# A mixer block with a product-key expert layer: U and V stages of the experts run as one mixed stage

## Reference

```
q = (h @ peer_wq).reshape(T, 8, 2, 128)
s = einsum('thpd,hpkd->thpk', q, peer_keys)        # 128 scores per head and side
sv, si = top_k(s, 16)
cand = sv[..., 0, :, None] + sv[..., 1, None, :]   # 16 x 16 pairs
top, pos = top_k(cand, 16)                         # 16 experts per head and token
eidx = i * 128 + j of the chosen pair;  g = softmax(top)
a = gelu(einsum('td,thkd->thk', h, peer_u[eidx]))
out = einsum('thkd,thk->td', peer_v[eidx], g * a)
x = x + ga2 * out
```

## Time and profile before

| | |
|---|---|
| median of 3 runs | 1783.68 us (1782.01 to 1784.19) |
| the profiled execution | 1786.27 us |
| its span, first to last instruction | 1784.5 us |
| TensorE busy | 1660.3 us (93%) |
| VectorE busy | 1420.8 us (80%) |
| ScalarE busy | 695.1 us (39%) |
| Pool busy | 607.4 us (34%) |
| moved by DMA | 443.82 MB, mean 249 GB/s |
| TensorE's granted clock, mean | 0.965 |

### The profile page before, as it was taken

The page is one execution under the profiler, slowest core; times in us unless marked ns, Lnnn a source line. Parts: engine busy times, 40 slices in busy tenths (PEclk is TensorE's granted clock), DMA queues, the critical chain, the costliest instruction groups (busy, mean ns, idle before and its releaser), DMA issues.

```text
span 1784.5 us, 29098 instructions
## 1 busy us (share of the span) xinstructions
PE 1660.3 (93%) x9345; PEld 1510.1 (85%) x9345; DVE 1420.8 (80%) x2563; ACT 695.1 (39%) x987; POOL 607.4 (34%) x633
## 2 busy tenths in 40 slices
PE   2899889999899996899898899899999999999998
PEld 1675447887688996798898898899999999999998
DVE  7795646657599999988898898865888888888886
ACT  4331655233434333254454454443333333333331
POOL 2100000101234554555555555541333333333331
PEclk8999789999999998899999999999999999999999
DMA  7521114655322554488898998988999999999996
GB/s 248 175 95 36 60 41 152 222 187 189 118 83 96 178 170 131 153 290 329 320 338 335 336 335 322 357 300 318 341 343 352 349 338 350 354 336 349 354 339 227
DMA packets 182381, 443.82 MB, mean 249 GB/s; under 512 B 13728, under 2 KB 95776, under 8 KB 180656
## 3 DMA queue, kind: packets, MB, share of 16 engines
q1 hardware_dynamic: 118768, 234.91, 38.4%
q0 software_dynamic: 42784, 156.26, 23.6%
q10 hardware_dynamic: 20768, 51.89, 7.8%
HBM read 388.47 MB, written 54.53 MB: 248 GB/s over the span
## 4 chain that ended last, share of the span: by engine, by line
PE 61%; DVE 24%; DMA 7%; issue 4%; ACT 3%; DVEq 0%; POOL 0%; ACTq 0%; POOLq 0%; SPq 0%
PE bank L1528 10%; PE bank L1527 10%; PE bank L1526 10%; PE bank L1278 8%; PE bank L1279 7%; PE bank L1280 7%; DMA sb_x<-u_rows_dram,sb_scr 4%; DVE sb_scr L1081 2%; DVE sb_wide L1184 2%; DVE sb_x L1145 2%; DMA a_scratch<-sb_scr 2%; PE bank L1501 2%; PE bank L1389 1%; DVE sb_scr L829 1%; DVE sb_w_lo L815 1%
## 5 line engine op out<-in xcount | busy, mean ns | idle before, releaser
L1278 PE MATMUL bank<-sb_act_hi,sb_w_hi 128*128 128x384 f32 (+1 forms) x1424 | 511.8, 359 | 14.4 <-POOL sb_w_lo L440 13.6
L1279 PE MATMUL bank<-sb_act_lo,sb_w_hi 128*128 128x384 f32 (+1 forms) x1424 | 503.1, 353 | 0.0
L1280 PE MATMUL bank<-sb_act_hi,sb_w_lo 128*128 128x384 f32 (+1 forms) x1424 | 503.0, 353 | 0.0
L497 ACT ACTIVATE sb_w_hi<-sb_stage 128x1024 fp32r<-128x1024 f32 x324 | 342.3, 1057 | 377.0 <-PE bank L1528 329.4
L815 DVE TENSOR_TENSOR sb_w_lo<-sb_stage,sb_w_hi 128x1024 fp32r<-128x1024 f32 x266 | 324.4, 1220 | 98.8 <-ACT sb_w_hi L497 92.2
L1528 PE MATMUL bank<-sb_mix_hi,sb_w_lo 128*128 128x384 f32 x1024 | 342.0, 334 | 0.0
L1527 PE MATMUL bank<-sb_mix_lo,sb_w_hi 128*128 128x384 f32 x1024 | 342.0, 334 | 0.0
L1526 PE MATMUL bank<-sb_mix_hi,sb_w_hi 128*128 128x384 f32 x1024 | 342.0, 334 | 0.0
L1278 PEld LDWEIGHTS bank<-sb_act_hi,sb_w_hi 128*128 128x128 f32 x1424 | 271.9, 191 | 36.6 <-POOL sb_w_lo L440 15.0
L1279 PEld LDWEIGHTS bank<-sb_act_lo,sb_w_hi 128*128 128x128 f32 x1424 | 271.9, 191 | 15.2 <-issue 0.5
L1280 PEld LDWEIGHTS bank<-sb_act_hi,sb_w_lo 128*128 128x128 f32 x1424 | 270.8, 190 | 15.9
(11 more groups left out here) (192 smaller groups left out, 1767.2 us busy)
## 6 DMA issues: line engine op xcount, KB each, us to landing
sb_stage<-u_dram SPq DMA_DIRECT2D x128, 512.0 KB, 3.9
sb_stage<-v_dram SPq DMA_DIRECT2D x128, 512.0 KB, 6.5
sb_stage<-w_front_dram SPq DMA_DIRECT2D x68, 512.0 KB, 3.3
a_scratch<-sb_scr ACTq DMA_DIRECT2D x128, 192.0 KB, 4.1
g_scratch<-sb_scr ACTq DMA_DIRECT2D x12, 2048.0 KB, 9.6
sb_scr<-g_scratch SPq DMA_DIRECT2D x32, 768.0 KB, 7.9
sb_scr<-a_scratch SPq DMA_DIRECT2D x32, 768.0 KB, 10.6
sb_scr<-w_ada_dram POOLq DMA_DIRECT2D x32, 512.0 KB, 4.4
```

What stands on the lines that cost most here:

```text
L497: nc.scalar.activation(w_hi[:, slot, :], stage[:, slot, :], ACT.Copy).then_inc(w_round, 1)
L1278: nc.tensor.matmul(out, w_hi[:, slot, w], rhs_hi[:, dc, :], start=(i == 0), stop=False)
L1279: nc.tensor.matmul(out, w_hi[:, slot, w], rhs_lo[:, dc, :], start=False, stop=False)
L1280: last = nc.tensor.matmul(out, w_lo[:, slot, w], rhs_hi[:, dc, :], start=False, stop=(i == len(dcs) - 1))
```

## The change

The two expert stages become one mixed stage. The first 64 U slabs (`EARLY`) stay on their own, then one more (`FUSED`); their coefficients still go through `a_scratch`. After that come 64 steps (`STEPS`), each of three units: the V slab of an early U slab, a new U slab (its gelu stays on the core), and the V slab of the new U slab of the step before. Four steps make a lap, for which SP loads G of four old and four new slabs and A of four old ones.

- V slabs are turned round: the coefficients are stationary and 512 weight columns move, 18 matmuls in six banks; the last two banks hold the new U slabs. At the end the three tiles' sums are copied out of PSUM and transposed.
- Pool splits the third unit of each step, VectorE the first two. Before the steps the G turns and the slabs up to `FUSED` + 2 are split by VectorE, as before.
- All gathers but eight move into the steps: four per step (two U rows, two V rows), issued by Pool behind its split, with eight row buffers and the index column read without a copy. Eight early dots are done in slabs 60 to 63. The last four steps have V rows only.
- The top-k is reordered: tiles 0 and 1 first (over all heads), with their lists after slabs 14 and 16, then tiles 2 and 3. The exponential is in slabs 9 and 34, the third list comes after the first G turn.
- G starts after slab 36 and is built in 24 slabs, two batches in each. It is laid out by groups of four slabs, so its store has runs of 512 bytes and its load runs of 6 KB; within a group the four slabs' values of a token lie together.
- `a_scratch` holds 64 slabs, not 128.

The core of the diff:

```diff
+EARLY = 64
+STEPS = SLABS - EARLY
+EXP_SLABS = {9: (0, 1), 34: (2, 3)}
+LIST_SLABS = (14, 16)
+G_FIRST = 36
+G_UNITS = 4
 G_TURNS = ND // (2 * TB)
 G_LAST = G_FIRST + G_TURNS * G_UNITS
 POOL_FIRST, POOL_LAST = WQ0 + 2, FRONT + G_FIRST + 2
-assert LIST_SLABS[-1] + 1 < G_FIRST and G_LAST < SLABS
-
-
-EARLY_SLAB = 28
-G_DOTS = 20
-DOTS_A = G_TURNS * G_DOTS
-LATE_TURNS = (SLABS - 4 - G_LAST) // 4
-LATE_DOTS = PICKS - DOTS_A
+LATE_LIST = DT - 1
+assert G_LAST <= EARLY - 4 and G_FIRST % RING == 0
...
+FUSED = FRONT + EARLY
+STEP0 = FUSED + 1
+LAP = 4
+LAPS = STEPS // LAP
+PICKS_LAP = PICKS // LAPS
+ROWS = 8
+EARLY_DOTS = PICKS_LAP
...
+            def lap_loads(lap, s, first=False, last=False):
+
+                def unit_load(c, src):
+                    slot = (STEP0 + c) % RING
+                    load(lap * (3 * LAP) + (STEP0 + c), slot, src).then_inc(w_in[slot], 16)
+
+                for k in range(LAP):
+                    unit_load(3 * k, v_d[bass.ds(lap * LAP + k, 1)])
+                    if k == 1 and not last:
+                        old_g(lap + 1, 1 - s, first)
+                        old_a(lap + 1, 1 - s, first)
+                    if not (last and k == LAP - 1):
+                        unit_load(3 * k + 1, u_d[bass.ds(lap * LAP + (EARLY + 1 + k), 1)])
+                    if first and k == 0:
+                        for i in range(2):
+                            sp.wait_ge(gw_out[i], 16 * G_TURNS)
+                        old_g(0, 0, True)
+                        old_a(0, 0, True)
+                        new_g(0, 0, True)
+                    if k == 2 and not last:
+                        new_g(lap + 1, 1 - s, first)
+                    if k == 1 and last:
+                        sp.wait_ge(c_mul, 2 * LAP * (LAPS - 1))
+                        sp.wait_ge(x2_out, 16)
+                        sp.dma_start(xend, x2_d.rearrange("c p t -> p c t")).then_inc(x2_in, 16)
+                    unit_load(3 * k + (1 if last and k == LAP - 1 else 2), v_d[bass.ds(lap * LAP + (EARLY + k), 1)])
...
+            def gather(g, which, k):
+
+                if g >= ROWS:
+                    pool.wait_ge(row_used, g - ROWS + 1)
+                pool.indirect_dma_start(row(g), None, v_rows_d if which else u_rows_d,
+                                        bass.IndirectOffsetOnAxis(ap=idx3[:, which, k:k + 1], axis=0)
+                                        ).then_inc(row_in[g % ROWS], 16)
+
+            for g in range(EARLY_DOTS):
+                if g == 4:
+                    pool.wait_ge(g_ok, ND // 4)
+                gather(g, 0, g)
+            g = EARLY_DOTS
+            for step_ in range(STEPS):
+                n = STEP0 + 3 * step_ + (1 if step_ == STEPS - 1 else 2)
                 split_unit(n, n % RING)
-            with pool.Fori(1, PICKS // 4) as t:
-                for b in range(4):
-                    u_gather(t, b)
-            v_rows_d = v_d.rearrange("j i d -> (j i) d")
-            for b in range(4):
-                pool.wait_ge(dot_ok, PICKS - 3 + b)
-                gather(1, b, b, v_rows_d)
-
-            def late_gathers(t):
-                for b in range(4):
-                    pool.wait_ge(acc_ok, t * 4 + (b - 2))
-                    gather(1, t * 4 + b, b, v_rows_d)
-
-            with pool.Fori(1, PICKS // 4) as t:
-                late_gathers(t)
+                for which in range(2):
+                    for k in range(2):
+                        pick = 2 * step_ + k + (0 if which else EARLY_DOTS)
+                        if pick < PICKS:
+                            gather(g, which, pick)
+                            g += 1
...
-                        nc.scalar.activation(gb[:, s, :, o:o + 4].rearrange("p j t -> p t j"),
-                                             bank[j % 4][:, :].rearrange("p (t j) -> p t j", t=4),
+                        nc.scalar.activation(gb[:, s, :, o:o + 4, :].rearrange("p a t b -> p t a b"),
+                                             bank[j % 4][:, :].rearrange("p (t a b) -> p t a b", t=4, b=4),
                                              ACT.Copy).then_inc(g_cp, 1)
                         if o == TB - 4:
 
                             act.wait_ge(g_cp, it * (2 * TB // 4) + (j + 1))
-                            act.dma_start(g_d[bass.ds(it * 2 + s, 1)].rearrange("a p n -> p (a n)"),
-                                          gb[:, s, :, :].rearrange("p j t -> p (j t)")).then_inc(gw_out[s], 16)
+                            act.dma_start(g_d[:, :, bass.ds(it * (8 * TB) + 4 * TB * s, 4 * TB)].rearrange("a p n -> p a n"),
+                                          gb[:, s, :, :, :].rearrange("p a t b -> p a (t b)")).then_inc(gw_out[s], 16)
 
...
+            def c_high(idx, pos, unit):
+
+                act.wait_ge(c_mul, idx + 1)
+                act.wait_ge(w_used, unit - 3 * LAP + 1)
+                nc.scalar.activation(mix_hi[:, pos % C_RING, 0:ND], cf[:, pos % 2, :], ACT.Copy).then_inc(c_hi, 1)
+
+            def gelu_new(q, par, unit):
+                act.wait_ge(w_used, unit + 1)
+                nc.scalar.activation(ga[:, par, :], bank[6 + par][:, 0:ND], ACT.Gelu).then_inc(ge_ok, 1)
...
+                def round_at(c):
+                    if not (last and c > 3 * LAP - 2):
+                        round_unit(act, (unit(c), lap * (16 * 3 * LAP // RING) + 16 * ((STEP0 + c) // RING + 1)), (STEP0 + c) % RING)
+
+                for k in range(LAP):
+                    idx = lap * (2 * LAP) + 2 * k
+                    round_at(3 * k + 3)
+                    c_high(idx + 1, 2 * k + 1, unit(3 * k + 2))
+                    if last and k == LAP - 1:
+                        break
+                    round_at(3 * k + 4)
+                    c_high(idx + 2, 2 * k + 2, unit(3 * k + 3))
+                    round_at(3 * k + 5)
+                    if isinstance(lap, int) and lap == 0 and k == 0:
+                        act.wait_ge(a_out[1], 16 * EARLY // 2)
+                    else:
+                        act.wait_ge(c_mul, idx)
+                    gelu_new(None, (k + 1) % 2, unit(3 * k + 1))
...
+            for h in range(PH):
+                for tt in range(2):
+                    topk(tt, h)
+            for tt in range(2):
+                below_top(tt)
+            for tt in range(2):
                 for part in range(3):
-                    indices(at_, (GT + at_) % TT, part)
-
-
-            dve.wait_ge(ht_cp, 2)
-            dve.wait_ge(ijt_cp, 3 * DT)
+                    indices(tt, part)
+            for tt in range(2, TT):
+                for h in range(PH):
+                    topk(tt, h)
+                below_top(tt)
+            for tt in range(2, TT):
+                for part in range(3):
+                    indices(tt, part)
...
+            def dot(slot, turns, par, k):
+
+                dve.wait_ge(row_in[slot % ROWS], turns * 16)
+                nc.vector.tensor_tensor_reduce(row(slot), row(slot), htok[:, :], 1.0, 0.0, ALU.mult, ALU.add,
+                                               dot8[:, par, k:k + 1]).then_inc(row_used, 1)
+
+            def accumulate(slot, turns, seen, k):
+
+                dve.wait_ge(row_in[slot % ROWS], turns * 16)
+                if seen is None:
+                    dve.wait_ge(acc_zero, 1)
+                else:
+                    dve.wait_ge(row_used, seen)
+                nc.vector.scalar_tensor_tensor(out=acc, in0=row(slot), scalar=w8[:, k:k + 1], in1=acc,
+                                               op0=ALU.mult, op1=ALU.add).then_inc(row_used, 1)
...
+            def new_product(idx, pos, turns, s, k, gelus):
+                dve.wait_ge(new_in[s], turns * 16)
+                dve.wait_ge(ge_ok, gelus)
+                c_product(idx, pos, ga[:, k % 2, :], g_new[s][:, :, k])
...
+                for k in range(LAP):
+                    idx = lap * (2 * LAP) + 2 * k
+                    new_product(idx + 1, 2 * k + 1, turns, s, k, lap * LAP + (EARLY + k + 1))
+                    take(2 * k)
+                    split_at(3 * k + 3)
+                    c_low(idx + 1, 2 * k + 1)
+                    if not (last and k == LAP - 1):
+                        if k < LAP - 1:
+                            old_product(idx + 2, 2 * k + 2, turns, s, k + 1)
+                        else:
+                            old_product(idx + 2, 2 * k + 2, turns1, 1 - s, 0)
+                    take(2 * k + 1)
+                    if not (last and k >= LAP - 2):
+                        split_at(3 * k + 4)
+                    if not (last and k == LAP - 1):
+                        c_low(idx + 2, 2 * k + 2)
+                    if k == 0:
+                        dve.wait_ge(g8_ok, lap + 1)
+                        nc.vector.tensor_tensor(w8, w3[:, bass.ds(lap * PICKS_LAP, PICKS_LAP)], g8, ALU.mult
+                                                ).then_inc(w8_ok, 1)
+                        dve.wait_ge(w8_ok, lap + 1)
+                    add(2 * k)
+                    add(2 * k + 1)
```

(65 more changed lines are left out.)

373 lines of the change are left out of this document (173 added, 200 removed).

## The result

| | before | after |
|---|---|---|
| median, us | 1783.3 (1782.0 to 1784.2, 4 runs) | 1961.0 (1957.4 to 1962.5, 4 runs) |
| span of the profiled execution, us | 1784.5 | 1959.1 |
| ratio | | 1.0994, 95% interval 1.0975 to 1.1013 |

The changed kernel is 9.9% slower; 7% was forecast. Four stages of the changed kernel, cut at its own events, answer to the earlier trace rows: window, us, busy us (instructions) of TensorE's matmuls, its weight loads, VectorE, ScalarE, Pool, then the granted clock, the DMA share and GB/s.

A forecast was written before the change was run, and what follows sets the result against it. TensorE bound the old V stage, DMA close behind; a four-engine loop was to bind the mixed steps. 965 + 60 x 14.8 + 4 x 12.3 + 12 = 1,914 us span, so 1,913 us, 7% slower; range 1,810 to 1,995 us.

The forecast's parts named there:

- The step: Mixed stage: each of 60 steps takes 14.8 us, above TensorE's 12.3, so TensorE idles 2.5 us in each.
- landing: Mixed step: a gather takes 6.2 us from issue to landing, between 5.2 at light traffic and 7.3 in the V stage.
- the product with G four words apart: VectorE in the mixed step: reading G at that stride adds 0.3 us, at most 0.69.
- the loop: Mixed step: Pool's split, gather, landing, VectorE's dot and split, back to Pool's split; once round takes 14.8 us.
- Tiles 0 and 1 are 16 of them, 98 us, to 577 us: Before G: VectorE's top-k of these tiles, 16 (head, tile) pairs, takes 98 us from 479.4 us and ends at 577 us.
- All before 562.5 us is unchanged: Start of the kernel: everything up to the first U slabs at 562.5 us keeps its earlier times.
- the G stage: First G matmul at 761 us; 24 slabs at 7.16 us to 930 us; with allowances, mixed steps start at 965 us.
- the stage before 965 us ending past 1,010 us: Sign of a wrong prediction: the stages ahead of the mixed steps end past 1,010 us, not at 965 us.
- TensorE sets the step (12.3 us): Rival for the mixed step: the loop does not bind, step 12.3 us, total 1,764 us, 1.1% faster; chance 0.08.
- VectorE full through the lock at 12.7 us: Rival for the mixed step: gathers early, VectorE full with Pool's split blocking it, 12.7 us, total 1,788 us; chance 0.04.
- Fast landings of 5.2 us: Rival: the loop binds but gathers land in 4.9 to 5.2 us, step 13.2 to 13.5, total 1,818 to 1,836; chance 0.15.
- the slow stores of the DMA rival: Rival: 512 B stores make G slabs 9 us, 44 us more; steps near 16, total 2,010 to 2,030 us; chance 0.13.

The follow-up runs named there:

- experiment 2: Changed kernel with Pool issuing a step's four gathers ahead of its split, not behind it: 1827.7 us, 1.0235 of before.
- experiment 3: Changed kernel with Pool issuing a step's two V-row gathers ahead of its two U-row gathers: 2177.7 us (one run).
- experiment 4: Changed kernel with VectorE splitting all three slabs of a step and Pool only gathering: 1829.6 us, 1.0244 of before.
- experiment 5: Changed kernel with VectorE taking both dots of a step behind its second split and low part, Pool's order unchanged: 1822.1 us (one run).
- experiment 1: Changed kernel with VectorE's wait for the rank table moved behind the top-k of tiles 0 and 1: 1892.1 us, 1.061 of before.

## Why the prediction was right, and where a step failed

The time came out 48 us above the forecast, within the range. That it stayed within is in part luck: the upper end was set for slow gathers, which did not come, and what used it up was a delay that the prediction did not have. Laid out on the span (1,914 forecast, 1,959 measured), the sums are: up to the mixed steps 1,017 for 965 (Pool's first split), 60 steps 887 for 888, the rest 55 for 61.

**The step: right.** 14.79 us for 14.8. Term by term: landing 5.9 us median (4.9 to 6.5 for the rows in `sb_x`, the first buffer) for 6.2; Pool's split 2.56 to 2.58 us for 2.46; the product with G four words apart 0.28 us longer (0.83 against 0.55) for 0.3; VectorE's part from dot to end of the second split 5.86 us (1511.34 to 1517.20) for 5.9 with the stride. Traffic of 286 GB/s meets the 287 from which the landing was picked, which follows from the step and is no second proof; and traffic alone does not give the landing (see the last section). Experiments 2, 3, 4 and 5 each open or stretch another arc of the loop (Pool's order, the issue, the split's owner, VectorE's order), and each moved the step in the direction that a loop asks for, experiment 3 by 1 us more than expected. One reading beside the sum was off: TensorE waits 1.6 us a step where 2.5 was said. It is busy some 13.3 us a step (826.42 us over 920), not 12.3, at a mean granted clock of 0.96; the loop hides it. The rule that the Trainium skill has for a strided source (Vector Engine (DVE) Microarchitecture Reference, 5.2) gives an estimate of 0.26 us, worked out from its row for a source that hops 4 KiB with every element; here the hop is four words, and the trace agrees with 0.28 us.

**Failed step: "Tiles 0 and 1 are 16 of them, 98 us, to 577 us".** "All before 562.5 us is unchanged" and the top-k's start at 479.4 us were carried over from before, while the wait for the rank table had moved ahead of it. Measured: start at 561.6 us, ScalarE held 50.9 us, TensorE 43.9 us, first G matmul 817.6 us instead of 761. Experiment 1 confirms it: with the wait behind the top-k it is 752.5 us. The other terms up to there were thus too dear, by 8 us on balance. From the first G matmul on, the G stage gave back 5 us more to Pool's first split, so the mixed steps came 52 us late. The prediction had named this as a sign of being wrong, "the stage before 965 us ending past 1,010 us", and it came. The end gave back 6 us: the last three distances of Pool's splits, with the loop open, are 11.35, 11.77 and 8.2 us, and 23.6 us remain after the last.

**G stage: right in length, in part by luck.** From the first G matmul to the first V matmul 202 us (817.6 to 1019.8) for 204. But 14 of the 204 were allowances for G stores and the late list, and the time went elsewhere: the last G matmul is at 988.8 us, and the five slabs behind it, reckoned at 21 us, took 31, with a wait of 8.5 us for VectorE's first low part. The stores in runs of 512 B were no burden in the stage: 8.9 us to land against 9.6 before. From 820 to 985 us their queue took 53.4% of 16 x 165 us for 48,400 packets, at most 0.029 us each, for an estimate of 0.034.

**The rivals.** That TensorE sets the step (12.3 us) is what experiment 2 brought about, at 12.39; in the changed kernel it did not hold. VectorE full through the lock at 12.7 us did not come either: with early gathers and Pool's split it stays at 659 of 700 us. The lock itself shows: a product of 8 elements, issued 0.23 us after Pool's split had started (1502.76 us, 2.58 us long), took 2.38 us and ended 0.03 us behind it:

```profile
1502.99 2.38 DVE L1340 TENSOR_TENSOR sb_scr<-sb_scr 128x8 f32<-128x8 f32 x1
```

The Trainium skill states that a VectorE instruction with two SBUF inputs contends with a Pool instruction that reads SBUF (SBUF — State Buffer, Who interferes with whom), and the trace agrees. But the block falls where VectorE has slack before its next wait. Fast landings of 5.2 us did not come, nor did the slow stores of the DMA rival.

**Open.** Single steps reach 16 us. Of those above 15.8 us all but the very first are a lap's last: that step takes 15.2 us on average, the other three 14.6. In it the second dot waits for its row too (start, us, line, form, and the wait with its releaser):

```profile
1544.85 1.23 DVE L1249 CUSTOM_DVE_ANT_0 sb_wide<-sb_wide,sb_htok 128x1024 f32<-128x1024 f32 x1 [0.57 <-DMA sb_wide<-u_rows_dram,sb_scr]
```

From the first dot to Pool's next split it is 6.8 us there and 6.0 in the others, a term that the prediction's sum did not have. SP issues a G and an A load of 768 KB in this step (1538.21 and 1538.89 us), in the middle of its four gathers (1535.05 to 1539.66 us); that they hold the row back is likely, but no run tries it. The price of the clock is not separated: the mean of 0.79 from 562 to 700 us (0.95 before in the same window) is part of what experiment 1 gave back.

## What to carry to other kernels

Before the durations, compare the order of waits on each engine, context lines of the diff too: a wait that stands still while work is moved behind it is a moved wait. When work of one engine is given to another, draw the loop from each handover back to itself over all queues it passes, and add it up; here a chain of 14.8 us set the step while the fullest engine needed 12.4. A loop is opened at its cheapest arc, by issuing what has a long landing first, or by placing what waits behind what others wait for, and no resource is needed for it.

## What the runs showed of the hardware that was not expected

- From 1050 us on, the first gather of Pool's four takes 1.76 us to issue in three steps of a lap and 0.95 in the second, the later ones 0.93 to 1.08. The second step of a lap is the one in which VectorE's product of 8 elements stands ahead of the adds, so that the first add starts with the gather (1505.50 and 1505.49 us) and not before it. In experiment 2 the first gather takes 1.39 us and the second 1.95. VectorE's adds ran beside both short and long ones; that it matters which of the two starts first fits these rows, but was not tried.
- From 1050 to 1750 us, median landings of the U rows grew from 5.9 to 7.9 us (first buffer) and from 5.7 to 6.7 us (second) in experiment 2, as traffic rose from 290 to 344 GB/s, and the step was 2.4 us shorter all the same. Traffic alone does not do it: at the same 344 GB/s they were 5.6 and 7.0 us in experiment 4, 6.2 and 6.0 in experiment 5.
- TensorE's granted clock fell to a mean of 0.79 of full speed over 562 to 700 us, the stretch with its pause of 43.9 us, and stood at 1.00 from 1050 to 1750 us in experiments 2 and 4, where TensorE never pauses.
